# Stage boundaries of a two-block transformer: norm scale and first transposes moved into the last part of the stage before, roots of the joined norms first on GpSimd, first two down tiles by column halves

## The reference

```python
def rmsnorm(x, g):
    return x * lax.rsqrt(jnp.mean(x * x, axis=-1, keepdims=True) + EPS) * g

for i in range(2):
    shift1, scale1, gate1, shift2, scale2, gate2 = split(cond @ ada_w[i] + ada_b[i], 6)
    h = rmsnorm(x, norm1_g[i]) * (1.0 + scale1) + shift1
    y = diff_attention(h, ...) if i == 0 else axial_gqa(h, ...)     # each ends in ... @ w_o
    x = x + gate1 * y
    h = rmsnorm(x, norm2_g[i]) * (1.0 + scale2) + shift2
    gate, up = split(h @ f_w_in[i], 2)                              # D_FF = 2816
    x = x + gate2 * ((silu(gate) * up) @ f_w_out[i])
x = rmsnorm(x, final_g)                                             # joined with the next norm
h = rmsnorm(x, mix_norm_g)
proj = h @ w_in            # 5888 columns; gating branch, attention branch, gates
x = x + merged @ w_out
h2 = rmsnorm(x, ffn_norm_g)
a, val = split(h2 @ w_up, 2)
x = x + (gelu(causal_depthwise_conv(a)) * val) @ w_down
out = rmsnorm(x, final_norm_g)
```

## Time and profile before

| what | value |
|---|---|
| runs | 1094.12, 1095.58, 1097.72; median 1095.58 |
| the profiled execution | 1093.62, its span 1091.9 |
| TensorE matmul busy | 1014.0 (93%) |
| VectorE busy | 740.0 (68%) |
| ScalarE busy | 541.7 (50%) |
| GpSimd busy | 53.3 (5%) |
| chain that ended last | TensorE 81%, VectorE 9%, ScalarE 4% |
| read from memory | 217.94 MB, 201 GB/s over the span |
| mean granted clock of TensorE | 0.988 |

### The profile page before, as it was taken

One profiled execution on the slowest core, in us unless ns is written; L12 is line 12 of the kernel. 1 busy time (PEld: TensorE's weight loads), 2 busy tenths in 40 slices (PEclk: granted clock), 3 DMA queues, 4 the chain that ended last, 5 costly groups with the idle time before them and its releaser, 6 DMA issues.

```text
span 1091.9 us, 12868 instructions
## 1 busy us (share of the span) xinstructions
PE 1014.0 (93%) x4808; PEld 834.4 (76%) x4808; DVE 740.0 (68%) x1041; ACT 541.7 (50%) x878; POOL 53.3 (5%) x92
## 2 busy tenths in 40 slices
PE   3599879999999999999999998999998899999997
PEld 2488667888878777777888786888787678888786
DVE  6788877877866798877765446646554567776753
ACT  1354655544443385666444445575545366555441
POOL 2100010000000410010000001000000000000000
PEclk9999989999999999999999998999999999999999
DMA  9798413998877855348866553756432347655551
GB/s 327 245 391 317 145 59 114 350 320 294 276 276 256 305 155 192 94 139 289 271 192 193 173 177 125 234 175 185 143 117 97 115 135 231 194 173 178 172 189 39
DMA packets 124790, 219.84 MB, mean 201 GB/s; under 512 B 9107, under 2 KB 77960, under 8 KB 124728
## 3 DMA queue, kind: packets, MB, share of 16 engines
q1 hardware_dynamic: 123440, 216.05, 60.1%
q0 software_dynamic: 960, 2.86, 0.9%
q10 hardware_dynamic: 328, 0.12, 0.0%
HBM read 217.94 MB, written 1.05 MB: 201 GB/s over the span
## 4 chain that ended last, share of the span: by engine, by line
PE 81%; DVE 9%; ACT 4%; issue 2%; DMA 2%; POOL 1%; DVEq 0%; SPq 0%; POOLq 0%; ACTq 0%
PE bank L1666 16%; PE bank L1668 16%; PE bank L1667 15%; PE bank L1681 5%; PE bank L1682 5%; PE bank L1683 5%; PE bank L1713 2%; PE bank L1714 2%; PE bank L1715 2%; PE bank L1768 2%; DMA ada<-in_ada_w 2%; ACT w_hi L548 1%; DVE ada_acc L1017 1%; DVE w_lo L994 1%; PE bank L1698 1%
## 5 line engine op out<-in xcount | busy, mean ns | idle before, releaser
L994 DVE TENSOR_TENSOR w_lo<-raw,w_hi 128x1024 fp32r<-128x1024 f32 x312 | 378.7, 1224 | 248.0 <-ACT w_hi L548 247.6
L548 ACT ACTIVATE w_hi<-raw 128x1024 fp32r<-128x1024 f32 x312 | 327.4, 1059 | 399.6 <-PE bank L1668 216.7
L1666 PE MATMUL bank<-w_hi,h_hi 128*128 128x512 f32 x768 | 306.1, 399 | 4.3 <-issue 4.1
L1668 PE MATMUL bank<-w_hi,h_lo 128*128 128x512 f32 x768 | 300.2, 391 | 0.0
L1667 PE MATMUL bank<-w_lo,h_hi 128*128 128x512 f32 x768 | 299.6, 390 | 0.0
L1666 PEld LDWEIGHTS bank<-w_hi,h_hi 128*128 128x128 f32 x768 | 144.7, 188 | 34.6 <-issue 5.6
L1668 PEld LDWEIGHTS bank<-w_hi,h_lo 128*128 128x128 f32 x768 | 144.5, 188 | 31.0
L1667 PEld LDWEIGHTS bank<-w_lo,h_hi 128*128 128x128 f32 x768 | 144.8, 189 | 29.0 <-issue 0.5
L1681 PE MATMUL bank<-w_hi,u_hi 128*128 128x512 f32 x216 | 85.6, 396 | 4.4 <-DVE act_u L1314 3.6
L1683 PE MATMUL bank<-w_hi,u_lo 128*128 128x512 f32 x216 | 84.1, 390 | 0.0
L1682 PE MATMUL bank<-w_lo,u_hi 128*128 128x512 f32 x216 | 84.1, 389 | 0.0
(11 more groups left out here) (275 smaller groups left out, 1199.6 us busy)
## 6 DMA issues: line engine op xcount, KB each, us to landing
ada<-in_ada_w SPq DMA_DIRECT2D x96, 512.0 KB, 5.8
raw<-in_f_w_in SPq DMA_DIRECT2D x176, 256.0 KB
raw<-in_w_in SPq DMA_DIRECT2D x46, 512.0 KB
raw<-in_f_w_out SPq DMA_DIRECT2D x44, 512.0 KB
raw<-in_w_up SPq DMA_DIRECT2D x88, 256.0 KB
raw<-in_a_w_qkv SPq DMA_DIRECT2D x24, 512.0 KB
raw<-in_w_down SPq DMA_DIRECT2D x22, 512.0 KB
raw<-in_b_w_qkv SPq DMA_DIRECT2D x12, 512.0 KB
```

The lines of the kernel that those rows point to most:

```text
L548: nc.scalar.activation(w_hi[:, m % SPL], raw[:, m % RAW], ACT.Copy).then_inc(hi_done, 1)
L994: ve.tensor_tensor(w_lo[:, m % SPL], raw[:, m % RAW], w_hi[:, m % SPL].bitcast(F32), ALU.subtract).then_inc(lo_done, 1)
L1666: mm(o, hi, w_hi[:, s, k], start=(u == 0 and k == 0), stop=False)
L1668: last = mm(o, lo, w_hi[:, s, k], start=False, stop=(u == 3 and k == 1))
```

## The change

On TensorE, `half_transposes` of the first token half is called from inside the last part (1, 1), after the second of its four tiles, through a new argument `mid`; at all five boundaries. On ScalarE the first token half's scale and its first two pieces come ahead of the split of a weight tile. On VectorE the scale comes ahead of `part_residual` of (1, 0), and piece 0 ahead of that of (1, 1). GpSimd's `root(3)` of the joined norms stands ahead of a wait for the end of the stage and of two loads; its first two steps wait only for the squares of `x` (new semaphore `part_sx`), and the third for those of `xn`. In the gated feed-forwards, the first two down tiles run column half 1 of both, then column half 0 of both (`half_tall`).

```diff
--- before.py
+++ after.py
@@ -275,6 +275,7 @@
         part_x = sem("part_x")
         part_y = sem("part_y")
         part_sq = sem("part_sq")
+        part_sx = sem("part_sx")
         root_ok, root_x = sem("root_ok"), sem("root_x")
         scaled_a, scaled_d = sem("scaled_a"), sem("scaled_d")
         merge_ok = sem("merge_ok")
@@ -455,24 +456,26 @@
 
             def root(r, with_y=False):
 
-                for t in range(T):
-                    pool.wait_ge(part_sq, 4 * r + 2 * t + 2)
-                    mean, mean_y, first, second = (stat[:, c + t:c + t + 1] for c in (MEAN + t, MEAN_Y + t, ROOT, ROOT_Y))
-                    after = stat[:, MEAN + 2 * t + 1:MEAN + 2 * t + 2]
-                    after_y = stat[:, MEAN_Y + 2 * t + 1:MEAN_Y + 2 * t + 2]
-                    nc.gpsimd.tensor_scalar(first, mean, after, EPS, ALU.add, ALU.add).then_inc(pre_tmp, 1)
+                def step(op):
+
+                    op.then_inc(pre_tmp, 1)
                     power[0] += 1
                     pool.wait_ge(pre_tmp, power[0])
+
+                for t in range(T):
+                    mean, after, mean_y, after_y, first, second = (stat[:, c:c + 1] for c in (
+                        MEAN + 2 * t, MEAN + 2 * t + 1, MEAN_Y + 2 * t, MEAN_Y + 2 * t + 1, ROOT + t, ROOT_Y + t))
                     if with_y:
-                        nc.gpsimd.tensor_scalar(second, first, EPS, mean_y, ALU.mult, ALU.add).then_inc(pre_tmp, 1)
-                        power[0] += 1
-                        pool.wait_ge(pre_tmp, power[0])
-                        nc.gpsimd.tensor_scalar(second, second, after_y, None, ALU.add).then_inc(pre_tmp, 1)
-                        power[0] += 1
-                        pool.wait_ge(pre_tmp, power[0])
+                        pool.wait_ge(part_sx, 2 * t + 2)
+                        step(nc.gpsimd.tensor_scalar(first, mean, after, EPS, ALU.add, ALU.add))
+                        step(nc.gpsimd.tensor_scalar(second, first, EPS, mean_y, ALU.mult, ALU.add))
+                        pool.wait_ge(part_sq, 4 * r + 2 * t + 2)
+                        step(nc.gpsimd.tensor_scalar(second, second, after_y, None, ALU.add))
                         nc.gpsimd.tensor_tensor(second, second, half[:, 0:1], ALU.pow).then_inc(root_ok, 1)
                         nc.gpsimd.tensor_tensor(first, first, half[:, 0:1], ALU.pow).then_inc(root_x, 1)
                     else:
+                        pool.wait_ge(part_sq, 4 * r + 2 * t + 2)
+                        step(nc.gpsimd.tensor_scalar(first, mean, after, EPS, ALU.add, ALU.add))
                         nc.gpsimd.tensor_tensor(first, first, half[:, 0:1], ALU.pow).then_inc(root_ok, 1)
 
             norm(0)
@@ -517,10 +520,10 @@
 
             pool.wait_ge(mm_done, IN_1 + 4)
             pool.dma_start(row[:], final_g.partition_broadcast(P)).then_inc(late_in[1], 16)
+            root(3, with_y=True)
             pool.wait_ge(mm_done, IN_C)
             pool.dma_start(mask_sb[:], masks).then_inc(late_in[2], 16)
             pool.dma_start(gmlp_row[:], gmlp_g[0].partition_broadcast(P)).then_inc(late_in[2], 16)
-            root(3, with_y=True)
             pool.wait_ge(gm_sq, 1)
             inv_sqrt(0, 2, 768).then_inc(gm_r, 1)
             root(4)
@@ -576,7 +579,7 @@
                     nc.scalar.activation(xn[:, t, span], x[:, t, span], ACT.Square, scale=1 / 32,
                                          accum_out=mean).then_inc(part_sq, 1)
                 else:
-                    nc.scalar.activation(xs[:, t, span], x[:, t, span], ACT.Square, scale=1 / 32, accum_out=mean)
+                    nc.scalar.activation(xs[:, t, span], x[:, t, span], ACT.Square, scale=1 / 32, accum_out=mean).then_inc(part_sx, 1)
                     act.wait_ge(part_y, 2 * t + n + 1)
                     nc.scalar.activation(merged_b[:, 2 * t + n], xn[:, t, span], ACT.Square, scale=1 / 32,
                                          accum_out=stat[:, MEAN_Y + 2 * t + n:MEAN_Y + 2 * t + n + 1]).then_inc(part_sq, 1)
@@ -614,12 +617,12 @@
                 first = nxt - SKEW + SPL
                 for n in range(2):
                     part_square(r, 0, n)
-                split(first)
                 part_scale(r, 0)
                 if shift is not None:
                     act.wait_ge(gain_ok, r + 2)
                 part_operand(o, 0, 0, gain, shift)
                 part_operand(o, 0, 1, gain, shift)
+                split(first)
                 part_square(r, 1, 0)
                 part_square(r, 1, 1)
                 part_operand(o, 0, 2, gain, shift)
@@ -1135,10 +1138,10 @@
                 part_residual(r, s, nxt, 0, 1, gated)
                 if before is not None:
                     before()
+                part_scale(r, 0)
                 part_residual(r, s, nxt, 1, 0, gated)
-                part_scale(r, 0)
+                part_operand(o, 0, 0, gain, shift)
                 part_residual(r, s, nxt, 1, 1, gated)
-                part_operand(o, 0, 0, gain, shift)
                 part_operand(o, 0, 1, gain, shift)
                 low(first)
                 part_operand(o, 0, 2, gain, shift)
@@ -1683,6 +1686,19 @@
                         last = mm(o, lo, w_hi[:, s, n], start=False, stop=last_k)
                 last.then_inc(mm_done, 1)
 
+            def half_tall(m, a_hi, a_lo, k, n, first=False):
+
+                pe.wait_ge(lo_done, m + 1)
+                s = m % SPL
+                for t in range(T):
+                    o = bank[2 * n + t][:]
+                    hi, lo = (h[:, k, t * P:(t + 1) * P] for h in (a_hi, a_lo))
+                    mm(o, hi, w_hi[:, s, n], start=first, stop=False)
+                    mm(o, hi, w_lo[:, s, n], start=False, stop=False)
+                    last = mm(o, lo, w_hi[:, s, n], start=False, stop=False)
+                if n == 0:
+                    last.then_inc(mm_done, 1)
+
             def first_wide(m0, o, src):
 
                 for t in range(T):
@@ -1701,11 +1717,13 @@
                         if t == T - 1:
                             last.then_inc(mm_done, 1)
 
-            def part_tall(m0, a_hi, a_lo, k0, count, t, n, base=0, only=False, last_k=True, wait_low=None):
+            def part_tall(m0, a_hi, a_lo, k0, count, t, n, base=0, only=False, last_k=True, wait_low=None, mid=None):
 
                 for j in range(count):
                     if wait_low is not None:
                         wait_low(j)
+                    if mid is not None and j == count // 2:
+                        mid()
                     pe.wait_ge(lo_done, m0 + j + 1)
                     s = (m0 + j) % SPL
                     out_ = bank[base + 2 * n + t][:]
@@ -1717,11 +1735,12 @@
                         last.then_inc(mm_done, 1)
                 return last
 
-            def last_tall(m0, a_hi, a_lo, k0, count=SKEW, base=0, only=False, between=None):
+            def last_tall(m0, a_hi, a_lo, k0, count=SKEW, base=0, only=False, between=None, mid=None):
 
                 for t in range(T):
                     for n in range(2):
-                        last = part_tall(m0, a_hi, a_lo, k0, count, t, n, base, only)
+                        last = part_tall(m0, a_hi, a_lo, k0, count, t, n, base, only,
+                                         mid=mid if (t, n) == (T - 1, 1) else None)
                         if (t, n) != (T - 1, 1):
                             last.then_inc(part_mm, 1)
                         if (t, n) == (0, 1) and between is not None:
@@ -1869,8 +1888,8 @@
                 pe.wait_ge(h_lo_ok, 4 * 1 + (4 if k == 1 else k // 2 + 1))
                 tall(WO_A + k, h_hi, h_lo, k, k == 0, False)
             pe.wait_ge(h_lo_ok, 4 * 1 + 4)
-            last_tall(WO_A + KD - SKEW, h_hi, h_lo, KD - SKEW, between=lambda: reduce_vector(4))
-            half_transposes(0, 0, xn)
+            last_tall(WO_A + KD - SKEW, h_hi, h_lo, KD - SKEW, between=lambda: reduce_vector(4),
+                      mid=lambda: half_transposes(0, 0, xn))
 
 
             def u_transpose(f, c, b, turn=None):
@@ -1881,7 +1900,7 @@
                                                    act_u[:, b, t, k * P:(k + 1) * P], ident[:])
                 last.then_inc(u_t, 1)
 
-            def feed_forward(base, f, v, gate_n):
+            def feed_forward(base, f, v, gate_n, then):
                 first_wide(base, v, xn)
                 for turn in range(5):
                     for j in range(LOOP):
@@ -1890,21 +1909,27 @@
                         wide(base + 4 + j, j % 4, 1 - j // 4, v, turn)
                         reduce_after(base + 4 + 8 * turn + j)
                 down = base + 4 * NCH_FF
-                for k in range(KF - SKEW):
+                pe.wait_ge(u_lo_ok, NCH_FF * f + 1)
+                for n in (1, 0):
+                    if n == 0:
+                        pe.wait_ge(u_ok, NCH_FF * (f + 1))
+                    for k in range(2):
+                        half_tall(down + k, u_hi, u_lo, k, n, first=k == 0)
```

(23 more changed lines are left out.)

## The result

The changed kernel takes 1088.26 (nine runs, 1087.11 to 1092.89), the kernel before 1097.69 in nine runs that include the three shown above. The ratio is 0.993, 95% interval 0.9918 to 0.9942: 7.7 us faster by it, 6.4 to 9.0. (The two medians lie 9.4 apart, the two means, 1096.57 and 1088.86, lie 7.7 apart.) The profiled execution took 1088.02, its span 1086.3, against 1091.9. A second measurement beside other kernels gave 0.9941 (0.9922 to 0.996).

A forecast was written before the change was run, and what follows sets the result against it. TensorE's queue, busy 93% of the span, was taken as the bound. Terms -2.7 + 0.3 - 0.2 - 3.9 = -6.5 (-6.6 with rounding), from 1095.58, gave 1089.0; forecast 1087 to 1091, full range 1085.5 to 1092.8.

The forecast's parts named there:

- The feed-forwards: First two down tiles of both gated feed-forwards: 1.36 us of each wait for act_u filled, -2.7 together.
- both bounds' question: Gain per gated feed-forward between 0, if the next thing is as late, and 1.36 us.
- B0 to B2: First three boundaries: end 0.05, 0.2 and 0.05 us later, put at +0.3 together.
- steps (a) to (d): At boundary 1: scale earlier; next stage starts at 386.0, not 387.27; waits 0.95 and 0.3; second scale later, end 0.2 later.
- step (c): At boundary 1, VectorE's last residual starts 1.07 us later, so TensorE waits 0.95 for piece 1 and 0.3 for piece 2.
- B3: Boundary 3: earlier root brings the fourth group of matmuls from 680.86 to 676.95, -3.9 us; bounds -2 and -4.7.
- The clock's share: At boundary 3, some 2 us of the 3.9 gain come from TensorE no longer falling to 1.2 GHz.
- The clock assumption: At boundary 3, TensorE stays at 2.4 GHz, since a stop of 1.85 us elsewhere is followed by full pace.
- Rival C: Clock falls to 1.2 GHz at all five boundaries, 2.1 us each, 10.5 lost, time 1099.5; chance 0.04.
- Rival B: Gains given back: boundary 3 wins 2 instead of 3.9, feed-forwards lose 1.4, time 1092.3; chance 0.18.
- D: Change does nothing at boundary 3 because something else holds the root; time 1093.0; chance 0.07.

The follow-up runs named there:

- the swap: The changed kernel with the second token half's scale ahead of the fourth weight tile's w_lo subtraction on VectorE; 1087.97 in one execution.
- the run with four empty steps: The changed kernel with four empty GpSimd additions ahead of the first root's power at boundary 3; that boundary took 13.89 us, no whole time given.

## The prediction against the result

*The time.* 1089.0 was forecast and 1088.26 measured; 6.6 less was forecast and 7.7 (6.4 to 9.0) measured by the ratio. The base of the forecast, 1095.58 from three runs, lies lower than the 1097.69 of nine, so part of the nearness of the absolute figure is luck; by the stretches of one profile against another it is 6.38 for 6.5.

*The feed-forwards.* Right to two hundredths in size (1.36 and 1.38 for 1.36), and both bounds' question is answered: the whole 1.36 arrives, the gate's wait is 0.62 before and after, and the run with this part alone gives nothing back.

*B0 to B2, steps (a) to (d).* Each step came as written: at B1 0.15 lost in the middle of the last part, the next stage 1.22 earlier (forecast 1.27), waits of 0.8 (forecast 0.95) and then 0.3 in front of the second and third pieces, and the fourth group 0.05, 0.28 and 0.06 later. That VectorE's second scale is the bound is shown by the swap, which takes it away and wins 0.4 each. What step (c) missed is ScalarE's part: I took VectorE's queue behind the residual as the only chain, and the run with the second piece first shows a second one, residual, square, `hf`.

*B3.* -3.79 for -3.9, and its parts are sized by runs: 0.8 for the early steps of the root (0.77 in the sum); 4.6 for the root as a whole; and the order moved into the last part, which I had entered with the rest, costs 0.8 there. The prediction worked out the two new waits rightly (0.8 and 1.4; measured 0.78 and 1.25) but did not ask what B3 would be without them. The clock's share, "some 2 us", was read wrongly. TensorE does lose 2.1 at the lower clock in the kernel before, but more than half of that is lost while VectorE's chain would have held it up anyway. VectorE's two scales of B3, in the kernel before and with the root alone, whose clock stays at 1.00:

```profile
671.34 0.49 DVE L1103 TENSOR_SCALAR xs<-xn,stat 128x512 f32<-128x512 f32 x1 [3.75 <-POOL stat L473]
...
679.58 0.48 DVE L1103 TENSOR_SCALAR xs<-xn,stat 128x512 f32<-128x512 f32 x1
```

```profile
667.04 0.48 DVE L1106 TENSOR_SCALAR xs<-xn,stat 128x512 f32<-128x512 f32 x1
...
674.86 0.48 DVE L1106 TENSOR_SCALAR xs<-xn,stat 128x512 f32<-128x512 f32 x1
```

From the start of the last part to the first scale it is 6.09 before (671.34 - 665.25) and 2.26 with the root alone (667.04 - 664.78): 3.8 of the 4.6 are the root's lead. From there to the fourth group it is 9.52 (680.86 - 671.34) and 8.76 (675.80 - 667.04): the other 0.8. With the root alone VectorE also stands 0.2 for the end of the last part, so the clock's share is 0.8 to 1.0 by these rows (an estimate). The -3.9 does not hang on it, for it was added up along VectorE's chain.

*The clock assumption.* Its outcome was right, its ground was wrong, as the run with four empty steps and the one below show. Rival C did not come about: nothing in B0 to B4 ran at the lower clock after the change.

The Trainium skill, TensorE: Matmul & The Clock Gate, Part 1 (HAM oscillation), was taken above to speak against the change. The kernel it tells of waits longer for its loads than this one does in its changed boundaries, so the rule was stretched to short stops; taken so, they would have to bring the clock down again and again. The traces show a fall behind stops of 1.77, 1.96, 3.12 and 3.98, none behind stops of 1.85 and 1.78 in the kernel before, and none behind the change's own of 0.78 and 1.25. The measurement decides here: the repeated short stops of the changed boundaries did not bring the clock down.

*Rival B and D.* Out: nothing was given back, and the root was the cause at B3.

## What to carry to other kernels

Moving work into the stage before does not shorten a boundary if the engine that finishes the boundary waits for that stage's end; look for the instruction that releases the end of the boundary (here the second half's scale, behind a weight tile that nobody needed yet) and move that one. A wait at the head of an idle engine's queue, like GpSimd's ahead of two loads, can cost more than anything on the busy engines, so read what stands behind each wait.

## What the runs showed of the hardware

A stop of TensorE of 1.77 us brought the clock down in one execution, and stops of 1.85 and 1.78 in another did not. In both feed-forwards of the kernel before, the matmuls behind the stops of 1.85 and 1.78 ran at full pace. In the run with the boundaries alone, whose feed-forwards are the same, the first took 7.58 behind its stop of 1.85, and the second 9.11 instead of 7.53. Its timeline and granted clock:

```profile
612.25 0.50 PE L1692 MATMUL bank<-w_hi,u_hi 128*128 128x512 f32 x1 [1.77 <-DVE act_u L1325]
...
613.78 0.63 PE L1694 MATMUL bank<-w_hi,u_lo 128*128 128x512 f32 x1
```

```profile
612.25:616.00 3.75, 3.75 (x11) 2.94 (x12) 0.40 (x1) 1.06 (x1) 0.00 (x0) 0.62 0.41 140
```

The matmuls follow each other at 0.43 instead of 0.23. So the stops that the halves removed can have a price beyond their length. Three profiles have these stops, two each (the run with the root alone is the third), and the clock fell behind one of the six; behind none in the ten profiles with the halves. How often it occurs beyond these was not measured.

The executions of one kernel spread by some 3 us, and one place of it is in the opening. The stretch from the first weight matmul to B0's last part took 136.3 in the kernel before and 138.6 in the run of the halves alone, which is the same code up to there. The granted clock around the first attention heads, of this run, then of the kernel before:

```profile
120.00:125.00 5.00, 2.80 (x14) 1.50 (x12) 4.89 (x12) 2.73 (x11) 0.00 (x0) 0.91 0.72 222
125.00:130.00 5.00, 4.44 (x14) 2.19 (x14) 3.63 (x10) 3.83 (x16) 0.00 (x0) 0.50 0.04 14
```

```profile
120.00:125.00 5.00, 3.86 (x11) 1.71 (x11) 4.15 (x13) 4.35 (x17) 0.00 (x0) 0.66 0.63 203
125.00:130.00 5.00, 3.80 (x23) 2.43 (x24) 4.79 (x15) 3.52 (x13) 0.00 (x0) 1.00 0.00 0
```

The same stop there, 2.02 in front of `gate`, is followed by a longer or a shorter time at 0.50. Over all thirteen profiles this opening takes 136.2 to 138.9.

A second place is in the third block, between B3 and B4, where TensorE stops for 3.2 in every profile. Behind that stop six matmuls follow each other at 0.43 in the profile of the changed kernel, and twelve in the second profile of the same kernel. The stretch from the end of B3 to the start of B4 takes 207.75 in the one and 209.04 in the other, and six times 0.2 is nearly that difference. Both places are as large as most of the terms of the sum, which is why the parts are told by stretches and not by whole times.
